# A twelve-layer fp32 transformer kernel: gate and up products with both activation halves in one 512-column matmul

## The reference, cut to what matters

```
def swiglu(h, w_gu, w_down):                       # layers 0 to 3
    g, u = jnp.split(h @ w_gu, 2, axis=-1)
    return (jax.nn.silu(g) * u) @ w_down

def channel_sublayer(x, n2, w_gu, cw, cb, w_dn):   # layers 4 and 5
    h = rms_norm_2(x, n2)
    g, u = jnp.split(h @ w_gu, 2, axis=-1)
    g = depthwise_conv_centred(g, cw, cb)          # 3 taps over the tokens
    return x + (jax.nn.gelu(g, approximate=False) * u) @ w_dn
```

## Time and profile before

| what | value |
|---|---|
| median of 3 runs | 2474.38 us (2473.13 to 2476.92) |
| the profiled execution | 2475.91 us |
| its span, first to last instruction | 2474.1 us |
| TensorE busy, share of the span | 2322.7 us, 94% |
| TensorE weight loads | 2205.0 us, 89% |
| DVE busy | 1541.5 us, 62% |
| ACT busy | 1202.0 us, 49% |
| mean granted TensorE clock | 0.962 of full speed |

### The profile page before, as it was taken

The page is one execution under the profiler, slowest core; times in us unless marked ns, Lnnn a source line. Parts: engine busy times, 40 slices in busy tenths (PEclk is TensorE's granted clock), DMA queues, the critical chain, the costliest instruction groups (busy, mean ns, idle before and its releaser), DMA issues.

```text
span 2474.1 us, 55862 instructions
## 1 busy us (share of the span) xinstructions
PE 2322.7 (94%) x23102; PEld 2205.0 (89%) x23102; DVE 1541.5 (62%) x2361; ACT 1202.0 (49%) x2025; POOL 55.6 (2%) x83
## 2 busy tenths in 40 slices
PE   6799899999999989899987998999998999998998
PEld 5689799999999978799976897999997999897998
DVE  6644355566565568565577543555685777775776
ACT  5533454455544436454455334544575544675443
POOL 1000000000000000000010000000000000000000
PEclk8889999999999989999998899999999999999999
DMA  4220155543455423255522201555433455333553
GB/s 174 94 87 4 44 189 178 178 136 125 158 187 177 146 93 103 94 173 175 195 77 94 86 4 37 191 173 188 144 113 111 160 181 185 128 112 110 179 182 122
DMA packets 88436, 327.21 MB, mean 132 GB/s; under 512 B 9808, under 2 KB 9936, under 8 KB 87632
## 3 DMA queue, kind: packets, MB, share of 16 engines
q1 hardware_dynamic: 87984, 322.72, 38.7%
q0 software_dynamic: 288, 2.10, 0.2%
HBM read 323.73 MB, written 1.05 MB: 131 GB/s over the span
## 4 chain that ended last, share of the span: by engine, by line
PE 83%; DVE 9%; ACT 5%; issue 2%; DMA 0%; ACTq 0%; DVEq 0%
PE bank L1887 16%; PE bank L1888 15%; PE bank L1889 15%; PE bank L1909 5%; PE bank L1910 4%; PE bank L1911 4%; DVE w_split L2091 2%; PE bank L435 2%; ACT w_split L1982 2%; PE bank L444 1%; PE bank L1303 1%; PE bank L1878 1%; PE bank L1305 1%; PE bank L1304 1%; PE bank L458 1%
## 5 line engine op out<-in xcount | busy, mean ns | idle before, releaser
L1887 PE MATMUL bank<-h_split,w_split 128*128 128x256 f32 x3168 | 915.8, 289 | 23.7 <-DVE w_split L2091 8.9
L1888 PE MATMUL bank<-h_split,w_split 128*128 128x256 f32 x3168 | 900.4, 284 | 0.0
L1889 PE MATMUL bank<-h_split,w_split 128*128 128x256 f32 x3168 | 899.9, 284 | 0.0
L2091 DVE TENSOR_TENSOR w_split<-ring_a,w_split 128x1024 fp32r<-128x1024 f32 x468 | 561.2, 1224 | 252.0 <-ACT w_split L1982 250.7
L1887 PEld LDWEIGHTS bank<-h_split,w_split 128*128 128x128 f32 x3168 | 607.1, 192 | 36.2 <-issue 18.5
L1888 PEld LDWEIGHTS bank<-h_split,w_split 128*128 128x128 f32 x3168 | 602.3, 190 | 1.6
L1889 PEld LDWEIGHTS bank<-h_split,w_split 128*128 128x128 f32 x3168 | 601.2, 190 | 0.0
L1982 ACT ACTIVATE w_split<-ring_a 128x1024 fp32r<-128x1024 f32 x468 | 477.1, 1049 | 62.8 <-PE bank L1889 40.4
L1909 PE MATMUL bank<-act_split,d_split 128*128 128x256 f32 x1008 | 285.7, 283 | 5.3 <-DVE act_split L2162 2.9
L1910 PE MATMUL bank<-act_split,d_split 128*128 128x256 f32 x1008 | 285.1, 283 | 0.0
L1911 PE MATMUL bank<-act_split,d_split 128*128 128x256 f32 x1008 | 285.0, 283 | 0.0
(11 more groups left out here) (276 smaller groups left out, 3357.2 us busy)
## 6 DMA issues: line engine op xcount, KB each, us to landing
ring_a<-wa SPq DMA_DIRECT2D x474, 512.0 KB, 4.2
ring_d<-wd SPq DMA_DIRECT2D x132, 512.0 KB, 4.2
tab_sb<-tab SPq DMA_DIRECT2D x1, 2448.0 KB, 13.6
hT<-na POOLq DMA_DIRECT2D x2, 1024.0 KB, 6.1
xT<-x SPq DMA_DIRECT2D x1, 1024.0 KB, 5.0
out<-xT SPq DMA_DIRECT2D x1, 1024.0 KB, 3.9
vec_sb<-vec SPq DMA_DIRECT2D x1, 288.0 KB, 5.0
tab_sb<-tab SPq DMA_DIRECT2D x1, 65.0 KB, 4.7
```

The costliest lines, as they stand in the source:

```text
L1887: mm(dst, w[:, 0, ks], x[:, 0, k, :], start=(k == 0), stop=False)
L1888: mm(dst, w[:, 0, ks], x[:, 1, k, :], start=False, stop=False)
L1889: last = mm(dst, w[:, 1, ks], x[:, 0, k, :], start=False, stop=(k == KT - 1))
L2091: v.tensor_tensor(w_split[:, u % 4, 1, :], ring_a[:, u % 4, :], w_split[:, u % 4, 0, :].bitcast(f32), ALU.subtract).then_inc(s["w_lo"], 1)
```

## The change

In the ffn alone, gate and up products take a high weight block once for both activation halves: one matmul with 512 moving columns (high and low activation side by side, through a strided view) writes a whole bank; the low-weight matmul then adds 256 columns to the bank's first half. So the first half of a bank ends up with two of the three products and the second half with the third, and the halves are summed on evacuation. Gate and up of a tile now fill a bank each: banks 4 and 5 for q = 0, banks 6 and 7 for q = 1. For the sum, ACT copies the second halves of both banks to `work` behind L2050 of the tile, DVE adds the first halves to them in two instructions, waits for both (`settle`), and multiplies the sums by the inverse rms in one instruction as before, but from `work` in SBUF. The wait on `a_used` (the products are done) moves from DVE to ACT, and DVE waits on the new `low_sums`. Down products, weight splitting, loads and all mixers stay.

```diff
+            def wide_unit(L, n, i, bank, first):
+
+                pe.wait_ge(s["w_lo"], i * 4 + (L["us"] + n + 1))
+                w, both = w_split[:, (L["u"] + n) % 4, :, :], bank[:, :].rearrange("p (a b) -> p a b", a=2)
+                for k in range(KT):
+                    if first:
+                        pe.wait_ge(s["h_ready"], 8 * L["hs"] + k + 1)
+                    ks = slice(k * P, (k + 1) * P)
+                    mm(both, w[:, 0, ks], h_split[:, :, k, :], start=(k == 0), stop=False, skip_group_check=True)
+                    last = mm(bank[:, 0:S], w[:, 1, ks], h_split[:, 0, k, :], start=False, stop=(k == KT - 1),
+                              skip_group_check=True)
+                last.then_inc(s["a_used"], 1)
...
                 def gate_up(i, q, first=False):
                     for g in range(2):
-                        unit(L, 2 * q + g, i, B[4 + q][:, g * S:(g + 1) * S], h_split,
-                             ready=("h_ready", 8 * L["hs"]) if first and g == 0 else None)
+                        wide_unit(L, 2 * q + g, i, B[4 + 2 * q + g], first and g == 0)
...
                             A(d_split[:, q, 0, :], ring_d[:, q, :], ACT.Copy).then_inc(s["dn_hi"], 1)
+                        if f or not isinstance(i, int) or i:
+                            act.wait_ge(s["act_ready"], i * 2 + (FT * f + q - 1))
+                        act.wait_ge(s["a_used"], i * 4 + (u + 2 * q + 2))
+                        A(work[:, 2 * q, :], B[4 + 2 * q][:, S:2 * S], ACT.Copy)
+                        A(work[:, 2 * q + 1, :], B[5 + 2 * q][:, S:2 * S], ACT.Copy).then_inc(s["low_sums"], 1)
...
-                        dve.wait_ge(s["a_used"], i * 4 + (u + 2 * q + 2))
-                        v.tensor_tensor(work[:, 2 * q:2 * q + 2, :], B[4 + q][:, :].rearrange("p (a b) -> p a b", a=2),
+                        dve.wait_ge(s["low_sums"], i * 2 + (FT * f + q + 1))
+                        for g in range(2):
+                            step.did(v.tensor_tensor(work[:, 2 * q + g, :], B[4 + 2 * q + g][:, 0:S],
+                                                     work[:, 2 * q + g, :], ALU.add))
+                        step.settle()
+                        v.tensor_tensor(work[:, 2 * q:2 * q + 2, :], work[:, 2 * q:2 * q + 2, :],
                                         inv_rms().unsqueeze(1).broadcast_to([P, 2, S]), ALU.mult)\
                             .then_inc(s["gu_ready"], 1)
...
-                with step.repeat(FT // 2 - 2, 4 if conv else 0, 1) as i:
+                with step.repeat(FT // 2 - 2, 8 if conv else 4, 1) as i:
```

More of the change, by code:

```diff
@@ L202, in build_program @@
                   "w_hi w_lo dn_hi dn_lo h_raw h_hi act_raw act_hi xm_raw xm_hi  o_hi o_ready "
-                  "gu_ready down_done squared out_done").split():
+                  "gu_ready down_done squared low_sums out_done").split():
             sems[n] = ctx.enter_context(nc.semaphore(n))
```

## The result

The changed kernel takes 2506.82 us (median of 4 runs, 2506.33 to 2507.29) against 2473.93 us for the kernel before (median of 4): a ratio of 1.0131, 95% interval 1.0116 to 1.0145. It is slower, as forecast, but by 33 us where 13 were forecast, and 5 us above the range, which ended at 2502. The profiled execution of the changed kernel took 2507.29 us and its span is 2505.5 us.

A forecast was written before the change was run, and what follows sets the result against it. TensorE was taken to bound both kinds of ffn, the conv ffn by a quarter of a microsecond. Conv ffns +36 and Silu ffns -23 gave +13 on 2475.9, 2489, or 2487.4 us as median; range 2475 to 2502.

The forecast's parts named there:

- the price of the wide matmul: TensorE, gate and up: 0.216 us wide plus 0.120 narrow, 0.336 per k block, saving 0.38 us a tile.
- the edges: Start and end of each Silu ffn: DVE's longer chain gives back 1.2 and 1.4 us of TensorE's 8.3 us saving.
- (a): Ffn matmuls: each pays the extra 13 ns, wide or narrow; 0.346 per k, 0.21 us saved a tile, 2501; chance 0.12.
- DVE's addition: Ffn evacuation: two additions from a bank and their settle add 0.92 us a tile in loops, 0.81 outside.
- (b): Ffn matmuls: the wide one costs two narrow ones, so nothing is saved; 2517 us; chance 0.06.
- (c): Ffn matmuls: loads disappear wholly, 0.320 per k, 0.63 us saved a tile; 2466 us; chance 0.06.
- (d): Conv ffns: DVE's additions vanish in its 0.5 us waits for ACT, tiles stay at 8.4 us; 2452; chance 0.05.
- (e): Changed ffn code: it doesn't do what it says, bank halves' flags or the loop's step count being off; chance 0.02.

The follow-up runs named there:

- loops-only kernel: Wide matmuls and split sums only in the loops of the four Silu ffns, the rest as in the kernel before: 2464.10 us against 2474.16, ratio 0.9954.

## Why the prediction was wrong

**The sign and the place were right.** Conv ffns slower because DVE's turn passes TensorE's, Silu ffns faster, `act_ready` late ahead of `down`, the clock unmoved at 1.00: all show. TensorE's idle time in a conv tile is 9.18 - 8.50 = 0.68 us, not 1.06.

**The step that failed is the price of the wide matmul**, the first term. It was put at 0.216 + 0.120 = 0.336 us a k block, from L1878; it is 0.233 + 0.118 = 0.351. L1878 is an fp32 matmul that runs as two instructions, each of which streams 256 columns in 0.216 us. I took that for the price of 512 column times of any kind. It shows that a load can hide behind 0.216 us, but not what 512 fp32r columns take: those need 0.231 to 0.235. The extra over the columns at 2.4 GHz is 11 to 13 ns for 256, 16 for 384, 18 to 22 for 512; and it went with the stream's length, not with the load, the layout or the neighbour. What sets L1878 apart, its data type or its running as two instructions, no run tested. So a tile saved 0.13 us, not 0.38. Silu ffns gained 0.35 us each, not 5.7, since of 22 x 0.13 = 2.9 us some 2.5 went at the edges: 21 us missing in four, where the forecast missed by 20. Rival (a) had this price nearly right (0.346) and missed by a few more nanoseconds in the saving that is left.

The trace of before also held a warning that the forecast did not use. It has fp32 matmuls of 512 columns, as two instructions each, at full granted clock:

```profile
1428.66 1.12 PE L547 MATMUL bank<-sq,tab_sb 128*128 128x512 f32 x2
```

From the first start to the second is 0.53 us, against 0.216 for the 256 columns of L1878: 2.5 times as long for twice the columns. A 512-column price scaled up from a shorter stream was thus not safe even within fp32.

**The edges were nearly right.** Forecast were 1.2 and 1.4 us. The waits of TensorE in the third ffn of the change (what waited, for whom, us in all, times, longest):

```profile
PE bank L1921 <- DVE act_last L2183: 1.3, 1, 1.3
PE bank L1921 <- DVE act_split L2183: 0.9, 1, 0.9
```

The 1.2 held 0.38 us of saving that TensorE can't use at the first edge; with the real 0.13 beside DVE's 0.8 it comes to the 0.9 measured. The balance above closes with these two to about 0.3 us. The loops-only kernel shows that the edges ate the saving: it keeps 2.4 us in each Silu ffn.

**DVE's addition was 0.92 us in the loop by forecast and is 0.79.** Two additions take 0.75, as worked out, but the settle behind them adds 0.04, not 0.15. The conv ffns lost 15.8 and 17.1 us, not 17.9 each: 33 instead of 36.

**Rivals.** (b), no saving, was too bleak: the wide matmul does take 10 us off. With narrow matmuls and the new evacuation the kernel takes 2517, which is (b)'s own number, but by luck: (b) added 36.5 us for the conv ffns and 6 for the Silu ffns, and the marks give 33 and 9. Its 1.5 us for a Silu ffn's edges is also less than the 0.81 + 1.4 = 2.2 that (a) and (c) are worked out with; 2.3 were measured. (c) rested on loads that hide. Halving them changed nothing, so they do hide, but the stream is slower than its columns. (d) fell: the additions don't hide. (e) did not come about: the change's matmuls and sums appear in the trace as written.

**The gap rule.** The Trainium skill (TensorE: Matmul & The Clock Gate, Back-to-back issue gap) gives 216 ns for 512 columns and 109 for 256. The measurements decide otherwise for fp32r: 512 columns took 233 ns here, and 256 took 118 to 120. The fp32 instructions of L1878 do take 216, but they stream 256 columns. The rule's conclusion, hardly any saving, came nearer the truth than my price did.

**The range** ended at 2502 because it reached (a) and stopped, and (b) was given 0.06. Both stood for the one unknown that no row showed, and together they deserved more than 0.18.

## What to carry to other kernels

Price a matmul from rows of its own data type and width: here 512 fp32r columns cost 233 ns where an fp32 instruction of 256 columns, which I took for the same length of stream, cost 216. Merging two matmuls that share weights saved only 8 ns in 359 here, and such a saving must be held against what the split accumulator adds on the engine that evacuates. Before adding work to an engine that shares a loop with the bound one, read how far its own turn lies below the bound in each kind of loop; the same 0.8 us was free in one and cost 0.8 us a tile in the other. And where a chain stands open at a loop's ends, use the longer form only inside.

## What the runs showed of the hardware

- An fp32r stream with full rows took 118 to 120 ns for 256 columns, 176 for 384 and 231 to 235 for 512, start to start at full granted clock. That is about 4 ns plus 0.445 ns a column, 7% over the 0.417 of 2.4 GHz; the line is a fit to these three widths. Half-size weight loads (64 columns) and a two-piece moving operand left it unchanged. Why it is so stays open.
- With 128 and 256 columns in turn, a pair took 229 ns, 61 and 168. That is about two loads at the 112 ns of 8-column matmuls.
- An fp32 matmul ran as two instructions: 216 ns each for 256 columns, 523 to 533 ns each for 512, both at full granted clock. Why the wider one takes 2.5 times as long stays open.
- DVE's multiplication with both inputs in SBUF took 1.95 us instead of 0.69 beside a GpSimd instruction that reads SBUF; its additions with one input in a bank kept their 0.76 us for two. A `tensor_scalar` of 128 x 256 took 1.25 instead of 0.41 there. GpSimd took 2.4 to 2.7 us for a subtraction of 128 x 1024 fp32 elements, which DVE does in 1.22.
